# Recurrence fills of a hybrid decoder step: the second of each pair moved into the slot of the first

## The reference

```
h = rmsnorm(x) * (1 + sc1) + sh1
q, f, i, og, glu_a, glu_b, gate_a, gate_b = split(h @ w_in + b_in)
S_t = diag(f_t) S_{t-1} + k_t v_t^T ;  o_t = S_t^T q_t        # per head, prompt from 0, samples from a state
o_a = rmsnorm_per_head(o) * norm_w * silu(og)
o_b = silu(layernorm(depthwise_conv31(glu_a * sigmoid(glu_b))))
x = x + g1 * (concat(sigmoid(gate_a) * o_a, sigmoid(gate_b) * o_b) @ w_out)
x = x + g2 * ((silu(gg) * uu) @ w_ffn_out)                    # gg, uu = split(h2 @ w_ffn_in)
y = rmsnorm(x)
```

## Time and profile before

| | us |
|---|---|
| median of 3 runs | 2081.59 (2078.96 to 2083.72) |
| the profiled execution, its own time | 2085.03 |
| its span, first to last instruction | 2083.3 |
| TensorE busy | 1985.6 (95%) |
| VectorE busy | 1249.4 (60%) |
| ScalarE busy | 659.6 (32%) |
| GpSimd busy | 263.3 (13%) |
| mean granted TensorE clock | 0.977 |

### The profile page before, as it was taken

How to read it: one execution, slowest core, us unless ns; L and a number is a source line. 1 busy time by engine, 2 the same in 40 slices (tenths; PEclk the granted TensorE clock), 3 DMA queues, 4 the chain that set the end, 5 groups by cost and what they waited for, 6 DMA issues and landing times.

```text
span 2083.3 us, 39204 instructions
## 1 busy us (share of the span) xinstructions
PE 1985.6 (95%) x15960; PEld 1901.7 (91%) x15960; DVE 1249.4 (60%) x1667; ACT 659.6 (32%) x1001; POOL 263.3 (13%) x217
## 2 busy tenths in 40 slices
PE   7699999999999999999869997999999999999997
PEld 3599999999999999998859997999999999999997
DVE  2786979796979787865463123654445544455544
ACT  2321313232222222233451113555333333333332
POOL 0520010100010101023243123920000000000000
PEclk9799999999999999999989997999999999999998
DMA  8412222222222222223162121444444444445442
GB/s 274 156 56 57 76 67 78 69 74 76 73 75 73 76 73 75 73 73 103 54 232 79 61 71 31 135 137 135 134 134 142 149 140 131 135 140 154 136 139 91
DMA packets 368856, 220.72 MB, mean 106 GB/s; under 512 B 15207, under 2 KB 360199, under 8 KB 368704
## 3 DMA queue, kind: packets, MB, share of 16 engines
q1 hardware_dynamic: 368720, 218.77, 35.4%
HBM read 195.49 MB, written 24.11 MB: 105 GB/s over the span
## 4 chain that ended last, share of the span: by engine, by line
PE 86%; DVE 6%; POOL 3%; DMA 2%; ACT 2%; issue 1%; SPq 0%; DVEq 0%; ACTq 0%; POOLq 0%
PE Z L772 76%; PE R L797 2%; PE R L853 1%; POOL mraw L2012 1%; PE R L719 1%; PE R L803 1%; POOL ysum L2005 1%; DMA ada_w<-in_w_ada_dram 1%; DVE ta L1315 1%; PE R L886 1%; PE R L879 1%; DVE x L1519 1%; DVE k L1179 1%; PE R L888 1%; DMA mraw<-merged_scratch 1%
## 5 line engine op out<-in xcount | busy, mean ns | idle before, releaser
L772 PE MATMUL Z<-h_hi,w_hi 128*128 128x352 f32 x2592 | 700.0, 334 | 24.7 <-POOL h_lo L1907 16.1
L772 PE MATMUL Z<-h_hi,w_lo 128*128 128x352 f32 x2592 | 676.4, 325 | 0.0
L772 PE MATMUL Z<-h_lo,w_hi 128*128 128x352 f32 x2592 | 674.9, 325 | 0.0
L1626 ACT ACTIVATE w_hi<-w_raw 128x1024 fp32r<-128x1024 f32 (+1 forms) x284 | 295.7, 1041 | 1002.1 <-PE Z L772 967.4
L1150 DVE TENSOR_TENSOR w_lo<-w_raw,w_hi 128x1024 fp32r<-128x1024 f32 (+1 forms) x260 | 318.8, 1227 | 312.7 <-ACT w_hi L1626 304.7
L772 PEld LDWEIGHTS Z<-h_hi,w_hi 128*128 128x128 f32 x2592 | 454.2, 190 | 46.3 <-issue 28.5
L772 PEld LDWEIGHTS Z<-h_hi,w_lo 128*128 128x128 f32 x2592 | 466.0, 190 | 0.0
L772 PEld LDWEIGHTS Z<-h_lo,w_hi 128*128 128x128 f32 x2592 | 464.9, 190 | 0.0
L1298 DVE SCALAR_TENSOR_TENSOR yb<-up,vec,yb 128x1024 f32 (+1 forms) x240 | 308.4, 1285 | 29.8 <-DVE yb L1298 3.7
L772 PE MATMUL Z<-act_hi,w_hi 128*128 128x352 f32 x528 | 170.3, 323 | 0.0
L772 PE MATMUL Z<-act_hi,w_lo 128*128 128x352 f32 x528 | 170.2, 322 | 0.0
(11 more groups left out here) (287 smaller groups left out, 2064.3 us busy)
## 6 DMA issues: line engine op xcount, KB each, us to landing
w_raw<-in_w_ffn_in_dram SPq DMA_DIRECT2D x132, 512.0 KB, 3.8
w_raw<-in_w_in_dram SPq DMA_DIRECT2D x64, 512.0 KB, 5.1
w_raw<-in_w_ffn_out_dram SPq DMA_DIRECT2D x48, 512.0 KB, 4.0
aw<-in_w_ada_dram SPq DMA_DIRECT2D x32, 512.0 KB, 4.2
w_raw<-in_w_ffn_out_dram SPq DMA_DIRECT2D x24, 384.0 KB, 3.4
mraw<-merged_scratch SPq DMA_DIRECT2D x16, 528.0 KB, 4.4
ada_w<-in_w_ada_dram SPq DMA_DIRECT2D x8, 1024.0 KB, 7.1
w_raw<-in_w_out_dram SPq DMA_DIRECT2D x16, 512.0 KB, 4.1
```

The costliest lines, as they stand in the source:

```text
L772: last = mm(out, w[:, kt, :], x(kt, g), start=first and kt == 0 and m == 0, stop=last_block and kt == n - 1 and m == 2)
L1626: A(w_hi[b.par][:, 0:n, :], w_raw[b.par][:, 0:n, :], ACT.Copy).then_inc(w_hi_ready, 1)
```

## The change

A table says which fills a slot issues: the first number of each of the five pairs gives both fills, the second gives none. The 25 fills keep their order, their banks and their counters; the readers on ScalarE and VectorE and the DMA queue are as before. The second fill of a pair moves one slot ahead, over 18 wide matmuls, and its old slot is left empty. In `LAST` the same holds; there `N_KV0` and `N_KV1` already stand in two slots after the same row.

```
+TOGETHER = {n + m: (n, n + 1) if m else () for n in (N_VT0, N_KT0, N_KV0, N_O0, N_OT0) for m in range(2)}
...
                 def slot():
                     n = fill_in_slot(at[0])
                     if rec and n is not None:
-                        rec_fill(n, h + (-1), f + n, lambda m: f + m)
+                        for m in TOGETHER.get(n, (n,)):
+                            rec_fill(m, h + (-1), f + m, lambda m: f + m)
                     at[0] += 1
...
                 if kind == "rec":
-                    rec_fill(m, Idx(NJ - 1), fill, rec7)
+                    for m in TOGETHER.get(m, (m,)):
+                        rec_fill(m, Idx(NJ - 1), rec7(m), rec7)
                     return
```

## The result

The changed kernel takes 2087.89 us (median of 12 runs, 2085.92 to 2093.63); the kernel before, timed beside it, 2083.37 us (12 runs, 2078.58 to 2086.22). The ratio is 1.0027 [1.0017, 1.0037]: slower by 0.27%, 4.5 us between the medians and 5.6 by the ratio. The forecast was 2085.1 us within 2080 to 2091, slower by 0.17%. Its sum was +3.5 us on the kernel before, and it was added to the median of the first 3 runs, 2081.6; the 12 runs beside the changed kernel have 2083.37.

A forecast was written before the change was run, and what follows sets the result against it. TensorE's own row of work was taken as the bound (86% of the span). Terms 0 + 9.7 - 1.8 - 4.4 = +3.5 us on the median 2081.6 gave 2085.1 us, range 2080 to 2091.

The forecast's parts named there:

- The reading of the table: All five pairs: the second fill was taken to be issued one slot earlier, in the first fill's slot.
- What a slot costs: TensorE switching between wide matmuls and a fill: 0 for the 40 moved fills, about -1 to +1 us in all.
- v, OT, KV and k pairs in heads: Heads 0 to 6: second fills one slot earlier find bank and input ready; KT1 waits at most a few tenths.
- O pair, +9.7 us: O1, issued behind O0, waits for VectorE's KV1 evacuation: 0.05 us in head 0, 1.4 or 1.8 in heads 1 to 6.
- Head 7's chain, -1.8 us: Head 7: KT1 earlier lets ScalarE's squares, GpSimd's adds and the token sums (`lnss`) come 1.8 us earlier.
- Clock relief, -4.4 us: Head 7: wait before the token sums shrinks from 4.2 to 1.3 us, so sums and following wide matmuls run at full clock.
- A wait of 1.3 us lies on the safe side: Head 7, before the token sums: the clock stays up, as after a 2.60 us wait; after 3.67 it had fallen.
- The clock relief does not come: Rival, head 7: clock still falls, so +9.7 - 1.8 = +7.9 us, 2089.5 us; chance 0.28.
- nothing to see: Rival: waits and gains cancel or are given back at a head's start, within 2 us of 2081.6; chance 0.08.
- The clock falls in every head: Rival: the clock drops in six heads, 1.3 us each, +7.6 on top, +11, 2092.7 us; chance 0.05.
- Faster: Rival: VectorE evacuates KV1 before q's readout, so O1 does not wait: -6.2 us, 2075.4 us; chance 0.08.

The follow-up runs named there:

- all_but_kv: Kernel before, with the first fill of the v, k, O and OT pairs one slot later, KV pair in two slots: 2085.50 us, ratio 0.9995.
- early_all_but_o: Kernel before, with the second fill of the v, k, KV and OT pairs one slot earlier, O pair in two slots: 2083.94 us, ratio 0.9990.
- early_pairs: Kernel before, with the second fill of all five pairs one slot earlier, the form the prediction describes: 2092.72 us, ratio 1.0047.
- k_early_head7: Kernel before, with KT1 issued one slot earlier, in KT0's slot, in head 7 only: 2083.53 us, ratio 0.9991.
- conv_slot9: Kernel before, with VectorE's convolution of the samples and the taps starting one slot later: 2082.30 us, ratio 0.9983.
- kv_pair_only: Kernel before, with only the KV pair issued in the later of its two slots: 2089.14 us, ratio 1.0021.

## Why the prediction was right or wrong

**The reading of the table: wrong.** This is the step that failed; the rest was reasoned on a kernel that wasn't the one timed. The prediction has O1 issued a slot early and waiting for the states, +9.7 us, and head 7 gaining 6.2. The runs show in place of both that KV0 comes a slot late, VectorE idles 1.2 to 1.6 us a head for it, and heads 1 to 6 grow by 0.8 to 1.0 us, +5.1 in all. That this lies near +3.5 is luck. A tuple evaluated by hand for one key, `N_KV0 + 0`, would have shown it. With the right reading the same rows led elsewhere: the question would have been who waits for a *first* fill that comes a slot late. The rows of before, shown above, answer it. KV1 starts at 765.70; with KV0's 8 passes in front of it the pair starts at 765.70 - 0.88 = 764.82 and has KV0 done at 765.70, 1.5 us after VectorE came for it at 764.18. Measured: 1.63.

**The missing mechanism.** The prediction costed a moved fill only by what TensorE waits for. A fill that comes later makes its reader idle, and what is queued behind the reader's instruction inherits it: 1.6 us of idle time at L1255 became 0.8 us on TensorE, 0.3 at O1 and 0.4 to 0.5 at OT2. This is shown: the loss comes with the KV pair alone, and goes when VectorE reads later, with TensorE's order unchanged.

**What a slot costs: right, as far as the runs tell.** In `all_but_kv`, with 32 empty slots, the seven distances sum to 748.7 against 749.2. Its timed interval, 0.9995 [0.9983, 1.0008], is wider than the 1 us of the prediction, from -3.5 to +1.7.

**v, OT, KV and k pairs in heads: right for the early form.** `early_all_but_o` has no O1 or OT1 wait in them; KT1 waits some 0.2 us in three heads, the "few tenths" that the prediction named, and all seven distances together are 1.2 us longer than before.

**O pair, +9.7 us: right for the form that it describes, not for the change.** In `early_pairs` the six waits are listed with 7.4 us, 1.2 to 1.3 each, and heads 1 to 6 grew by 1.5 to 1.9 each without the low-clock stretch, 9.8 in all. The form as a whole took more than the +3.5 forecast for it: its terms as measured give 9.8 + 1.3 (that stretch) - 0.2 (head 7's chain) - 4.1 (clock relief) = +6.8, and the timed 7.6 to 9.8 leave 1 to 3 us that no row places. In the real change VectorE's readout of q still stands in front of KV1, as the prediction said, but O1 keeps its slot and meets it by 0.2 to 0.3 us only.

**Head 7's chain, -1.8 us: mis-sized, and not part of the change.** In the real change KT1 keeps its slot, ScalarE still starts when it is done, and the sums wait 4.2 us as before. Where KT1 did move, the sums started 0.35 us earlier (`k_early_head7`) and 0.2 (`early_pairs`). The step took VectorE's and GpSimd's durations from the trace of before. Half of the 1.8 went to the longer L1182, and in `k_early_head7` 0.5 more to GpSimd's longer add (last section).

**Clock relief, -4.4 us: not part of the change** (0.50 in it from 1006 to 1009 us); in `early_pairs` it measured 4.1 against the 9.25 us of the profile before. Four other kernels with the same 4.2 us wait have 8.1 to 8.2 us there, though, against which it is 3.0: the term rests on one execution. "A wait of 1.3 us lies on the safe side" could not be tried, as the wait came out at 0.4 or 1.8; at 1.8 the clock did fall, later, and the relief was 2.6 by the same count, or 1.5.

**The rivals.** "The clock relief does not come" had +7.9, from an O1 wait that isn't in the change; "nothing to see" missed by more than its 2 us. "The clock falls in every head" did not happen: neither in the changed kernel, where the granted clock is 1.00 from 238 to 953 us, nor in `early_pairs` behind the O1 waits (1.00 from 781 to 793). "Faster" was rejected because VectorE's rows show work back to back, which was right, and it is what made a late KV0 dangerous. The Trainium skill ("Perfetto Trace Analysis", section Optimizing Tensor Performance, Matmuls) on the evacuation that another group's matmuls should cover: in the changed kernel KV0's evacuation stays covered and KV1's but for the 0.3 us that O1 loses. The loss begins with the evacuating engine's wait, which the rule doesn't speak of.

## What to carry to other kernels

Evaluate an index table for one key by hand before costing it; a pair moved earlier and a pair moved later have different victims. When a producer moves earlier, look for what it needs; when it moves later, look at its reader, and if that is an in-order engine that reached it without idle time, count how far behind everything queued after it falls, down to the next place where the producer needs it. Then consider moving the reader by the same amount: here this took the loss back in full, though it gained nothing on the kernel before.

## What the runs showed of the hardware

**VectorE and GpSimd slow each other, and the later one pays.** In `k_early_head7`, VectorE's L1182 (two inputs) started 0.13 us behind a GpSimd operation of 2.46 us and took 2.88 us; alone it takes 0.69. It ends 0.55 after GpSimd's. In the kernel before the two began within 0.01 us of each other, VectorE's took 0.69, and GpSimd's was the long one, 2.94 us, against 2.4 alone. The last row is that of `conv_slot9`, in which no fill moved:

```profile
963.24 0.69 DVE L1178 TENSOR_TENSOR qd<-qd,tot 128x512 f32<-128x512 f32 x1 [0.81 <-PE R L860]
963.85 0.69 DVE L1179 TENSOR_TENSOR k<-k,tot 128x512 f32<-128x512 f32 x1
963.84 2.94 POOL L1893 TENSOR_TENSOR w_lo<-w_raw,w_hi 128x1024 fp32r<-128x1024 f32 x1 [19.73 <-ACT w_hi L1626]
...
963.00 2.89 DVE L1179 TENSOR_TENSOR k<-k,tot 128x512 f32<-128x512 f32 x1
```

Of the eleven profiled kernels nine have GpSimd's operation 0.08 to 0.35 us ahead of VectorE's in this place, and VectorE's takes 2.88 or 2.89 us in all of them. Only before and in the changed kernel are the two within 0.05 us, and there GpSimd's takes 2.94 and 2.88. So a shift of a tenth of a microsecond decides whether GpSimd pays 0.5 us or VectorE 2.2. The short row that the prediction read was the exception, and moving KT1 is not what lengthened it. It took half of the gain that head 7 had been given. The Trainium skill ("SBUF — State Buffer", section Who interferes with whom) says that a VectorE instruction with two SBUF inputs contends with a GpSimd instruction that reads SBUF, by an exclusive lock, and that the order of issue decides which one blocks; the trace agrees.

**The clock after a short wait.** After the wait of 1.82 us the clock was still 1.00 for 3 us and then fell to 0.50, in all three kernels with such a wait (6.5 to 6.6 us from the sums to L894). To look at the first matmuls after a wait is not enough. After the 2.60 us in the earlier trace rows the granted clock stays at 1.00 up to 1110 us, further waits between, so the length of the wait alone doesn't decide. How long a low stretch lasts also varied in the same code. Between the two level fills behind the wait of 3.67 us (5.05 us before) it is 5.05 to 5.30 in seven of the eleven profiles and 6.05 to 6.32 in the other four, `early_pairs`, `kv_pair_only` and the two with KV0 read late. From the sums to L894 behind the wait of 4.2 us it is 9.24 or 9.25 in three and 8.12 to 8.17 in four. What decides that was not tried.
